# A transformer pair with experts: the second layer's projection cut into pieces and dealt out between its compression, latents and softmax units

## The reference, cut to what matters

```python
y = rms_norm(x, norm_g) @ w_in                       # 1024 -> 2744 columns
qc, kc, vc, ks, vs, kw, vw, gc, zc, cq, ckv, kr, zd = split_cols(y, CD_SPLITS)
qc = apply_rope(rms_norm(qc, c_q_norm), cos, sin)    # 8 heads of 64; ks, kw (2 heads) likewise
kc = nsa_compress(kc, pe[0], w1[0], w2[0])           # 15 blocks of 32 tokens: silu(flat @ w1) @ w2
vc = nsa_compress(vc, pe[1], w1[1], w2[1])           # kc is then normed and turned like ks
gates = sigmoid(gc)                                  # 8 heads x 3
# oc = g0 * softmax(q kc) vc + g1 * softmax(q ks) vs + g2 * softmax(q kw) vw
q  = rms_norm(cq, ..) @ d_w_uq                       # latent queries, 256 -> 8 x 96
kv = rms_norm(ckv, ..) @ d_w_ukv                     # latent keys and values, 128 -> 8 x 128
# od = softmax(norm(q) norm([k, kr])) v, causal, 8 heads
x = x + concat(oc * silu(zc), od * silu(zd)) @ w_out
```

## Time and profile before

| what | value |
|---|---|
| runs | 1054.78, 1049.28, 1044.74 us; median 1049.28 |
| profiled execution | 1048.44 us, span 1046.6 us |
| busy | TensorE 847.3, its weight loads 504.6, VectorE 307.1, ScalarE 166.1, GpSimd 36.0 us |
| HBM | 283 MB read, 271 GB/s over the span |
| layer CD | rows of tile 0 ready near 197 us, last values matmul of `attention(1)` 376 us |
| experts | from about 600 us to the end |

### The profile page before, as it was taken

How to read it: one execution, slowest core, us unless ns; L and a number is a source line. 1 busy time by engine, 2 the same in 40 slices (tenths; PEclk the granted TensorE clock), 3 DMA queues, 4 the chain that set the end, 5 groups by cost and what they waited for, 6 DMA issues and landing times.

```text
span 1046.6 us, 13223 instructions
## 1 busy us (share of the span) xinstructions
PE 847.3 (81%) x5629; PEld 504.6 (48%) x5629; DVE 307.1 (29%) x745; ACT 166.1 (16%) x444; POOL 36.0 (3%) x28
## 2 busy tenths in 40 slices
PE   5998888999776788999879899678686858767655
PEld 2445445444644675444554666435353535435432
DVE  1063772106135733401554222211201111111112
ACT  2013431101224332100321110000000000000001
POOL 0020000002002200000000000000000000000000
PEclk9999899999887679999999699988988888889889
DMA  9954483332440025544454599999999999999993
GB/s 349 389 196 174 156 281 126 110 133 74 168 162 0 1 79 199 187 180 160 168 235 173 229 394 418 428 425 428 428 428 426 427 426 426 428 428 427 427 427 161
DMA packets 52972, 284.68 MB, mean 272 GB/s; under 512 B 2608, under 2 KB 5040, under 8 KB 40112
## 3 DMA queue, kind: packets, MB, share of 16 engines
q1 hardware_dynamic: 52912, 283.80, 68.2%
HBM read 282.75 MB, written 1.05 MB: 271 GB/s over the span
## 4 chain that ended last, share of the span: by engine, by line
PE 54%; DMA 31%; DVE 7%; ACT 4%; issue 2%; POOL 1%; SPq 1%; DVEq 0%; ACTq 0%
DMA ring<-in_up_w 30%; PE banks L1441 28%; PE banks L1797 8%; PE banks L1520 3%; PE banks L1541 2%; PE banks L1468 2%; PE banks L1783 2%; PE banks L1505 1%; PE banks L1835 1%; DMA ring<-in_ab_w 1%; DVE mx L859 1%; PE banks L1411 1%; PE banks L1547 1%; PE banks L1673 1%; PE banks L1852 1%
## 5 line engine op out<-in xcount | busy, mean ns | idle before, releaser
L1441 PE MATMUL banks<-ring,hT 128*128 128x512 f32 (+2 forms) x704 | 293.4, 577 | 13.1 <-ACT hT L490 6.0
L1797 PE MATMUL banks<-ring,QT 128*32 128x256 f32 x1952 | 153.4, 464 | 88.5 <-DMA ring<-in_up_w 87.8
L1441 PEld LDWEIGHTS banks<-ring,hT 128*128 128x128 f32 x704 | 132.6, 191 | 167.4 <-issue 154.8
L1797 PEld LDWEIGHTS banks<-ring,QT 128*32 128x32 f32 x1952 | 85.9, 129 | 154.2 <-issue 127.8
L1337 DVE TENSOR_TENSOR QT<-banks,MOD 32x256 f32<-32x256 f32 x128 | 53.8, 420 | 138.0 <-PE banks L1835 136.7
L1835 PE MATMUL banks<-ring,QT 128*32 128x256 f32 x992 | 71.1, 434 | 14.3 <-issue 13.8
L1328 DVE TENSOR_TENSOR QT<-QT,banks 64x256 f32<-64x256 f32 x32 | 13.5, 423 | 212.6 <-ACT QT L704 212.6
L1783 PE MATMUL banks<-Y 128*128 128x128 f32 x256 | 65.4, 412 | 1.9 <-DVE Y L1314 1.1
L1783 PEld LDWEIGHTS banks<-Y 128*128 128x128 f32 x256 | 62.2, 334 | 8.3 <-issue 7.0
L465 POOL TENSOR_TENSOR rs<-st,mhalf 128x1 f32<-128x1 f32 (+5 forms) x19 | 29.6, 1561 | 1000.2 <-DVE st L753 532.0
L704 ACT ACTIVATE QT<-banks 64x256 f32<-64x256 f32 x32 | 12.0, 376 | 318.3 <-PE banks L1797 318.3
(11 more groups left out here) (301 smaller groups left out, 649.6 us busy)
## 6 DMA issues: line engine op xcount, KB each, us to landing
ring<-in_up_w SPq DMA_DIRECT2D x31, 2048.0 KB, 23.5
ring<-in_down_w SPq DMA_DIRECT2D x31, 2048.0 KB, 22.3
ring<-in_gate_w SPq DMA_DIRECT2D x30, 2048.0 KB, 19.1
ring<-in_ada_w SPq DMA_DIRECT2D x12, 2048.0 KB, 8.8
ring<-in_ab_w SPq DMA_DIRECT2D x5, 2048.0 KB, 19.7
ring<-in_cd_w SPq DMA_DIRECT2D x5, 2048.0 KB, 8.3
ring<-in_in_w SPq DMA_DIRECT2D x4, 2048.0 KB, 10.6
ring<-in_ab_out_w SPq DMA_DIRECT2D x2, 2048.0 KB, 9.9
```

The source lines that it names most:

```text
L1441: ins = pe.matmul(bank[j % 4][:, 0:n], hT[:, k, t * P:(t + 1) * P], w[:, k, :], start=(k == 0), stop=(k == KD - 1))
L1797: return pe.matmul(bank[1][CAP * j:CAP * j + CAP, 0:256], XG[q % 2][:, k, CAP * s:CAP * s + CAP], wk[:, :, 2 * (j % 2):2 * (j % 2) + 2], s ...
```

## The change

The columns of the projection are regrouped by first use: compression inputs and latent queries' input (512 columns); latent values' input, rope key, selected and window keys, gate logits (440); queries (512); selected and window values (256); the two output gates (512 each). Pieces of the projection are then placed between the steps that depend on earlier pieces. On TensorE the order is: pieces (0,0) (0,1) (1,0) as (chunk, tile); transposes of the compression inputs; (1,1); compression; (2,0); fold; transposes of the latents; (2,1); second compression product; latent values and queries; (3,0); key transpose; (3,1); transposes of keys and queries; (4,0) (4,1); compressed scores; two score units; compressed attention; eight units, each with a quarter of (5,0) or (5,1).

Roots and norms are split to match (`ROOTS` has now cdl0, cdl1, cdq0, kc, cdq1, dh0, dh1), squares are summed by ScalarE for the three latent inputs. The latents' sums, norms and rotations are all ahead of the softmax units, and GpSimd makes both tiles' gains after both roots. Compressed attention is block-diagonal: `kcT` holds the keys of group g in rows 64g to 64g+63 and columns 16g to 16g+15, zero elsewhere, so that one matmul has both groups; the probabilities of 8 heads by 16 are turned in one transpose; `vc_own` (VectorE) holds for each head its values in its own 16 rows and 64 columns, so that one matmul of 512 columns gives all heads. The silu of gate zc is made in taking chunk 4 from PSUM, that of zd after the units. The latent queries lie in `extra` and in a ring slot, which stays taken until the latent transposes are done.

The diff, cut (removed lines of the engines' parts stand in the kernel above):

```diff
@@ -33,11 +33,12 @@
             ("qi", 768, 256), ("va", 640, 128), ("vb", 2244, 128), ("za", 1092, 512), ("zb", 2372, 512),
             ("wi", 1088, 4)]
-CD_ORDER = [*((f"qc{h}", 64 * h, 64) for h in PAIRS), ("ks", 768, 128), ("kw", 1024, 128), ("kr", 2200, 32),
-            ("cq", 1816, 256), ("ckv", 2072, 128),
-            ("kc0", 512, 64), ("vc0", 640, 64), ("kc1", 576, 64), ("vc1", 704, 64),
-            ("vs", 896, 128), ("vw", 1152, 128),
-            ("zc", 1304, 512), ("zd", 2232, 512), ("gc", 1280, 24)]
+CD_ORDER = [("kc0", 512, 64), ("vc0", 640, 64), ("kc1", 576, 64), ("vc1", 704, 64), ("cq", 1816, 256),
+            ("ckv", 2072, 128), ("kr", 2200, 32), ("ks", 768, 128), ("kw", 1024, 128), ("gc", 1280, 24),
+            *((f"qc{h}", 64 * h, 64) for h in PAIRS), ("vs", 896, 128), ("vw", 1152, 128),
+            ("zc", 1304, 512), ("zd", 2232, 512)]
+CD_WIDTHS = [512, 440, 512, 256, 512, 512]
+CD_AT = [sum(CD_WIDTHS[:c]) for c in range(6)]
 def columns(order):
...
@@ -231,11 +237,14 @@
         add_cols("abin", ab_w, AB_N)
         add_ada(0, 7)
         add_cols("about", ab_out_w, D)
-        add_cols("cdin", cd_w, CD_N)
+        for c in range(3):
+            add_cd(c)
         chunks.append(("cmpw", [(0, SLOT, 32, cmp_w1)], ("cmp_hid", 1)))
         chunks.append(("lat", [(0, 1536, 2, rows(uq_w, 2)), (1536, 1024, 1, rows(ukv_w, 1)),
-                               (2560, 128, 2, cmp_w2)], ("uq_mm", 4)))
-        chunks.append(("scratch", [], ("d_scr", 2)))
+                               (2560, 128, 2, cmp_w2)], ("uq_mm", 3)))
+        for c in range(3, 6):
+            add_cd(c)
+        chunks.append(("scratch", [], ("dq_T", 8)))
         add_ada(7, 10)
         add_cols("cdout", cd_out_w, D)
         chunks.append(("rows", [(0, D, 1, norm_rows[:, 0:1]), (D, D, 1, norm_rows[:, 2:3])], ("final_row", 1)))
...
+                if name == "dh1":
+                    for t in range(NT):
+                        q3 = Dq[t].rearrange("p (h d) -> p h d", h=8)
+                        k3 = Dk[:, t, :].rearrange("p (h d) -> p h d", h=8)
+                        pool.wait_ge(*upto("l_norm", t + 1))
+                        pool.tensor_tensor(q3, q3, small("gain_dq").unsqueeze(1).to_broadcast([P, 8, 96]), ALU.mult)\
+                            .then_inc(sem("l_gain"), 1)
+                        pool.tensor_tensor(k3[:, :, 0:64], k3[:, :, 0:64],
+                                           small("gain_dk").unsqueeze(1).to_broadcast([P, 8, 64]), ALU.mult)\
...
@@ ScalarE: the tail of its part @@
+            take_cd(4, 0, 0, ACT.Silu)
+            take_cd(4, 1, 1, ACT.Silu)
             for t in range(NT):
                 act.wait_ge(*upto("gc", t + 1))
                 act.activation(gates[:, t, :], gates[:, t, :], ACT.Exp, scale=-1.0)\
                    .then_inc(sem("cd_ez"), 1)
             for t in range(NT):
                 act.wait_ge(*upto("c_shift", t + 1))
...
+                act.activation(tmp[:, 128 * t:128 * t + 128], tmp[:, 128 * t:128 * t + 128], ACT.Exp, scale=0.125)\
                    .then_inc(sem("c_exp"), 1)
...
+            def turned_compressed():
+                for t in range(NT):
+                    act.wait_ge(*upto("c_T", t + 1))
+                    act.activation(scrB[:, P * t:P * t + P], bank[4 + t][:, 0:P], ACT.Copy).then_inc(sem("c_Ta"), 1)
+            def output_gate(u):
+                n = u - U0[1]
+                if n % 4 == 3:
+                    take_cd(5, n // 4, 7)
+            attention(1, after=output_gate, early=turned_compressed)
+            for t in range(NT):
+                act.wait_ge(*upto("cdin_Pv" if t else "cdin_Pa", 6))
+                act.activation(cd_columns(5, t), cd_columns(5, t), ACT.Silu).then_inc(sem("cd_z"), 1)
             for j in range(0, 8, 2):
                 act.wait_ge(*upto("dq_T", j + 1))
                 act.activation(QT[0:96, 2 * j:2 * j + 2, :], bank[4 + j % 4][0:96, :], ACT.Copy)\
...
@@ VectorE: latents and compressed attention @@
+            query_sums(0)
+            rope_queries(0)
...
+            latent_sums(0)
+            latent_sums(1)
+            v.wait_ge(*upto("cdc_T", 2))
+            go(v.tensor_copy(QT[:, 0:2, :], bank[5][:, :]), "cdc_Tv")
+            latent_norm(0)
+            latent_norm(1)
+            latent_rope(0)
+            latent_rope(1)
...
+            def compressed_outputs():
+                for t in range(NT):
+                    compressed_sums(t)
+                for t in range(NT):
+                    v.wait_ge(*upto("c_pv", t + 1))
+                    link(v.tensor_tensor(heads(Y[:, t, 0:512], 8), heads(bank[6 + t][:, :], 8),
+                                         bc_dim(st[:, 24 * t + 16:24 * t + 24], 8), ALU.mult), "c_done")
+            for t in range(NT):
+                compressed_shift(t)
+            v.wait_ge(*upto("cdin_Pa", 5))
+            v.wait_ge(*upto("cdin_Pv", 5))
+            attention(1, early=compressed_outputs)
+            v.wait_ge(*upto("cd_z", NT))
...
@@ -1523,12 +1616,13 @@
                 if c is not None:
                     ada_sum(c)
...
+            def attention(part, ada=lambda u: None, fill=lambda u: None, early=lambda: None):
                 lo, hi = U0[part], U0[part + 1]
                 score_unit(lo)
                 score_unit(lo + 1)
+                early()
                 for u in range(lo, hi):
...
+                    finish_unit(u, hi, ada(u), fill)
             def ada_parts(c):
                 arrived(pe, f"ada{c}")
...
@@ TensorE: the whole new part @@
+            def project_cd(c, t, b, ks=range(KD)):
+                n = CD_WIDTHS[c]
+                if ks[0] == 0:
+                    arrived(pe, f"cdin{c}")
+                    if c > 0:
+                        pe.wait_ge(*upto("cdin_Pv" if t else "cdin_Pa", c))
+                w = weights(f"cdin{c}")[:, 0:KD * n].rearrange("p (k n) -> p k n", k=KD)
+                for k in ks:
+                    ins = pe.matmul(bank[b][:, 0:n], hT[:, k, t * P:(t + 1) * P], w[:, k, :],
+                                    start=(k == 0), stop=(k == KD - 1))
+                if ks[-1] == KD - 1:
+                    ins.then_inc(sem("cdin_mm"), 1)
+            def turn_into(b, srcs, name):
+                for i, src in enumerate(srcs):
+                    ins = pe.transpose(bank[b][:, P * i:P * i + P], src, ident)
+                ins.then_inc(sem(name), 1)
+            cd_rows = normed_rows("cd", "cdx")
+            for t in range(NT):
+                cd_rows(t)
+                project_cd(0, t, t)
+            project_cd(1, 0, 0)
+            pe.wait_ge(*upto("cdin_Pv", 1))
+            turn_into(4, tr(CD["kc0"]) + tr(CD["kc1"]), "cda_T")
+            project_cd(1, 1, 1)
             arrived(pe, "cmpw")
             pe.wait_ge(*upto("cmp_in", 5))
@@ -1611,74 +1721,96 @@
                 for odd in range(2):
                     for i in range(2):
                         r, o = slice(64 * i, 64 * i + 64), 64 * i + 32 * odd
...
+                        ins = pe.matmul(bank[5][o:o + 32, 0:128], cin[half][r, :, l % 16 + odd],
                                         w1[r, l + odd, :], start=(l == 0), stop=(l == 30))
             ins.then_inc(sem("cmp_hid"), 1)
+            project_cd(2, 0, 0)
+            pe.wait_ge(*upto("cmp_c", 1))
+            pe.matmul(bank[6][:, 0:64], tmp[:, 0:128], const("fold"), start=True, stop=True).then_inc(sem("cmp_t"), 1)
+            pe.wait_ge(*upto("cd_lat", 2))
+            cq = CD["cq"]
+            turn_into(7, tr(CD["ckv"]), "cdb_T")
+            turn_into(4, [Y[:, t, cq + k:cq + 256:2] for k in range(2) for t in range(NT)], "cdb_T")
+            project_cd(2, 1, 1)
             arrived(pe, "lat")
             lat = weights("lat")
+            pe.wait_ge(*upto("cmp_h", 2))
+            for g in range(2):
+                pe.matmul(bank[6][0:N_CMP, 64 + 64 * g:128 + 64 * g], hcT[:, 16 * g:16 * g + N_CMP], lat[:, 2560:2624],
+                          start=True, stop=True)
+            pe.matmul(bank[6][:, 192:256], hcT[:, 32:160], lat[:, 2624:2688], start=True, stop=True)\
+              .then_inc(sem("cmp_out"), 1)
+            pe.wait_ge(*upto("cdb_Tv", 3))
             for t in range(NT):
                 for half in range(2):
...
+                    pe.matmul(bank[2 + 2 * t + half][:, :], QT[:, 8, t * P:(t + 1) * P],
                               lat[:, 1536 + 512 * half:2048 + 512 * half], start=True, stop=True)\
                       .then_inc(sem("ukv_mm"), 1)
...
             uq = lat[:, 0:1536].rearrange("p (k n) -> p k n", k=2)
...
+            def latent_queries(out, t, cols):
+                for k in range(2):
+                    ins = pe.matmul(out, QT[:, 10 + k, t * P:(t + 1) * P], uq[:, k, cols], start=(k == 0), stop=(k == 1))
+                return ins
+            latent_queries(bank[7][:, :], 0, slice(0, 512)).then_inc(sem("uq_mm"), 1)
+            pe.wait_ge(*upto("d_a", 2))
```

(47 more changed lines are left out.)

354 lines of the change are left out of this document (162 added, 192 removed).

## The result

| | before | after |
|---|---|---|
| median of four runs each, us | 1049.96 | 999.67 |
| range | 1044.74 to 1054.78 | 995.68 to 1002.14 |
| profiled execution, span | 1048.44, 1046.6 | 1000.01, 997.8 |
| ratio, 95% interval | | 0.9528 [0.9495, 0.9561] |

The forecast was 1004 (995 to 1021) and faster. The page of after, DMA engines' busy tenths, answers to the earlier trace rows: the full stretch at the end is about as long (17 slices of 24.9 us, 16 of 26.2 before) and begins some 50 us earlier.

What follows compares the result with a forecast made beforehand. Expert-weight transfers bound the kernel from 620 us; ahead, a chain alternating between engines, with TensorE idle time and half clock to win. Part 1's end 376.0 - 329.9, less 0.5, gives 45.6; 1049.3 - 45.6 = 1003.7, taken as 1004, range 995 to 1021.

Steps and rivals of the forecast that it cites:

- the fixed point: Start of the second row tile's first matmul, 206.33 us in the profile of before; nothing before it was to change.
- Pieces at 0.842 ns a column: Projection on TensorE: a piece was to take 6.9 us at 512 columns, 5.9 at 440, 3.45 at 256.
- Compression taken at 6.3, gain at most 1: Compression on TensorE, between projection pieces: 6.3 us as before; up to 1 us from a better clock was taken as 0.
- Scores done: End of the compressed scores on TensorE: projection pieces and the work between them sum to 74.4 us, reaching 280.7.
- Late latents' chain, 1.1 us: Ahead of the compressed shift: latents' sums, roots, gains and rotations end at 280.9 instead of 279.8, 1.1 us late.
- Shift to first unit, 6.8: Compressed attention from shift start at 280.9 to TensorE turning the first unit's probabilities at 287.7.
- The price of the clock fall, 1.7: One fall of TensorE's clock for 3.4 us, after the idle time before the first unit, costs 1.7 us.
- Eight units 39.2, clock 1.7, handovers 1.3: Part 1's softmax units: 39.2 us of TensorE work, plus clock fall 1.7 and semaphore handovers 1.3, ending at 329.9.
- Tail +0.5: Behind part 1: late copies +0.6, Exp table load +1.3, latent transposes at full clock -1.4; together +0.5 us.
- The extra drain of 1.38 us on each load: ScalarE's table loads behind part 1: by the cited rule the tail's sum would be 1.4 us higher.
- Rest of the kernel unchanged, 45 us earlier: Behind the stage: the expert stretch keeps its length and begins 45 us earlier.
- the half clock in the units: Rival: softmax units stay at half clock, about 66 us instead of 39.2; total 1031, or 1017 for half the units; chance 0.13.

Runs made afterwards that it cites:

- e4: Kernel before plus two never-read 512-column matmuls in each of part 1's eight softmax units; units 44.5 us (before 50.8), ratio 0.9933.
- e5: Kernel before plus seven never-read 512-column matmuls, three at the wait for turned queries, four ahead of the compression; compression 3.73 us, ratio 1.0001.
- e6: Kernel after with the latents' norms and rotations on VectorE moved among part 1's softmax units; 995.6 us, ratio 0.9498.
- e10: Kernel after with the latents' four gains done on VectorE instead of GpSimd; 995.6 us, ratio 0.9480.
- e8: Kernel after plus two never-read 512-column matmuls behind the second compressed transpose; 995.7 us, ratio 0.9488.
- e1: Kernel after with the last chunk's projection (13.8 us) ahead of the compressed scores instead of between the softmax units; 1004.6 us, ratio 0.9573.

## Why the prediction was right, and where its sizes were off

The mechanism held: TensorE's own work bounds the stage in the new order, the pieces fill the waits, and what remains idle lies ahead of the first unit. That the old units lost time to the half clock is shown by e4, which takes 6.4 us out of them by adding work. By its steps, counted from the fixed point (forecast / measured):

- *Pieces at 0.842 ns a column*: held (6.87, 5.91, 3.45 in the chain).
- *Compression taken at 6.3, gain at most 1*: mis-sized by 2.65, it took 3.65. I wrote that no row shows a gain; but the granted clock of 0.50 from 282 to 286 us (under e5) could have been read in the trace of before. e5 shows that it was clock alone. Scores done: 74.4 / 71.2.
- *Late latents' chain, 1.1 us*: the shift started 1.3 us after the scores of the first tile were there; by e6 and e10 this is worth 1.2. VectorE lost 5.3 us beside the gains (L1009, L1010, L883, L884), more than I counted, and most of it was covered. This agrees with the rule cited from the Trainium skill (SBUF — State Buffer, Who interferes with whom): e10 takes GpSimd's share away, and the durations fall to the short ones.
- *Shift to first unit, 6.8*: 8.7. The values matmuls ran at half clock, 3.66 instead of 1.7 us. The price of the clock fall, 1.7, was right (e8: 1.7), its place was not: I had put it on the units, where it cost some 0.1 (37.05 us in after, 36.98 in e8).
- *Eight units 39.2, clock 1.7, handovers 1.3*: 42.2 / 37.0, the largest miss. TensorE never waits in these units, so the handovers cost nothing. The other 2.2 us lie in the sum: rows of groups in TensorE's queue overlap by some 0.15 us each (a wide unit's values are 1.89 long, and the next group starts 1.73 after them), and for transposes, scores and values I had added the row lengths.
- *Tail +0.5*: -0.6 to the end of the last D values (31.3 us behind part 1, 32.0 in before), and +0.1 to the start of the output projection, as the turning of the rows ahead of it took longer. The table load for Exp did not wait for the maximum. ScalarE of after, its two loads:

```profile
322.41 1.28 ACT L693 ACT_TABLE_LOAD   x1
323.70 1.15 ACT L693 ACTIVATE Y<-Y 128x512 f32<-128x512 f32 x2
...
328.02 1.28 ACT L535 ACT_TABLE_LOAD   x1
330.95 0.37 ACT L535 ACTIVATE PB<-banks,nmx 128x128 f32<-128x128 f32 x1 [1.65 <-DVE nmx L920]
```

The second load ends at 329.3 and ScalarE then waits 1.65 us: it ran in the idle time. The one load of the earlier trace rows had stood behind a wait of 5.71 us, and I took this for every load. The extra drain of 1.38 us on each load, for which I cited the Trainium skill (ScalarE: Activation LUTs, What ACT_TABLE_LOAD costs), does not appear: the silu starts at 323.70, right at the end of its load (322.41 + 1.28), and the load right behind the instruction ahead of it. Here the measurement decides.

- *Rest of the kernel unchanged, 45 us earlier*: 3.7 us were lost in it, 2.1 of them in the first group of the output projection; this is inside what the same instructions vary by between profiles.

Counted to the end of part 1, the scores came 3.2 us earlier than forecast (2.65 of it the compression), the units were 5.2 shorter, the shift began 0.2 later behind the scores, and from there to the first unit it was 1.9 longer: 6.4 us more gained than forecast. At the end of the kernel 3.2 are left. So it is in part luck that the total came so near to the forecast: 3.7 us were lost behind part 1, and no step of the prediction holds them. Of the rivals, the half clock in the units is the one that e1 brought about, by taking the pieces away; what stood against it in the prediction, one wide piece a unit, was the right reason.
